# Splitting the Fourier stage by even and odd frequencies, and moving conditioning sums between TensorE and VectorE

## What is computed

```python
sh_m, sc_m, gt_m, sh_f, sc_f, gt_f = jnp.split(silu_c @ w_mod[l] + b_mod[l], N_MOD, axis=-1)
f_x, q_x, k_x, v_x = split_even(modulate(x, g[0], sh_m, sc_m) @ w_in)
attn_x = window_attention(q_x, k_x, v_x, k_c, v_c, sink)
def fourier_mix(u):            # 4 groups of 256 channels, 256 tokens
    ug = u.reshape(b, n, 4, 256)
    return (jnp.fft.fft2(ug, axes=(1, 3)).real * (n * 256) ** -0.5).reshape(b, n, 1024)
mix_x = jnp.concatenate([fourier_mix(f_x), attn_x], axis=-1) @ w_out
```

## Time and profile before

| | |
|---|---|
| median of 3 runs | 2263.23 us (2260.5 to 2265.11) |
| the profiled execution | 2260.15 us, of which its span 2258.4 us |
| PE busy | 2197.8 us (97% of the span) |
| DVE busy | 1653.4 us (73%) |
| ACT busy | 1019.5 us (45%) |
| transfers | 592.63 MB, mean 262 GB/s |
| PE in the chain that ended last | 87% |
| granted clock, mean | 0.989 |

### The profile page before, as it was taken

One profiled execution on the slowest core, in us unless ns is written; L12 is line 12 of the kernel. 1 busy time (PEld: TensorE's weight loads), 2 busy tenths in 40 slices (PEclk: granted clock), 3 DMA queues, 4 the chain that ended last, 5 costly groups with the idle time before them and its releaser, 6 DMA issues.

```text
span 2258.4 us, 30977 instructions
## 1 busy us (share of the span) xinstructions
PE 2197.8 (97%) x11355; PEld 1806.4 (80%) x11355; DVE 1653.4 (73%) x1784; ACT 1019.5 (45%) x1269; POOL 97.7 (4%) x32
## 2 busy tenths in 40 slices
PE   6899999999999999999989999999999999999998
PEld 3478568788888888888868888887888888888887
DVE  0266767888788888888988889988888554654665
ACT  3163544554344345344454444446534443443443
POOL 0000000001010010110101101100011000000000
PEclk8899999999999999999999999999999999999999
DMA  9966978688888888889868788896887656666664
GB/s 374 352 224 226 373 273 298 231 295 278 302 275 285 290 272 292 294 275 318 291 213 279 272 298 280 275 310 226 288 286 247 198 193 189 188 193 193 205 195 149
DMA packets 253896, 592.63 MB, mean 262 GB/s; under 512 B 18082, under 2 KB 18610, under 8 KB 253234
## 3 DMA queue, kind: packets, MB, share of 16 engines
q1 hardware_dynamic: 253746, 590.63, 77.6%
HBM read 588.46 MB, written 2.10 MB: 261 GB/s over the span
## 4 chain that ended last, share of the span: by engine, by line
PE 87%; DVE 5%; DMA 4%; issue 2%; ACT 2%; SPq 1%; DVEq 0%; ACTq 0%
PE ps L520 30%; PE ps L526 15%; PE ps L595 11%; PE ps L596 11%; PE ps L597 11%; PE ps L559 2%; DMA early<-in_w_mod_dram 2%; DVE wlo L1276 1%; DMA mraw<-in_w_mod_dram 1%; DMA raw<-in_mlp_w_dram 1%; DVE acc L1286 1%; PE ps L481 1%; ACT whi L908 1%; DMA raw<-in_att_w_out_dram 1%; PE ps L687 0%
## 5 line engine op out<-in xcount | busy, mean ns | idle before, releaser
L1276 DVE TENSOR_TENSOR wlo<-raw,whi 128x1024 fp32r<-128x1024 f32 x712 | 901.0, 1270 | 429.1 <-ACT whi L908 427.7
L908 ACT ACTIVATE whi<-raw 128x1024 fp32r<-128x1024 f32 x712 | 751.7, 1059 | 946.9 <-PE ps L597 384.6
L520 PE MATMUL ps<-u,whi 128*128 128x512 f32 x2944 | 930.1, 397 | 9.8 <-DVE wlo L1276 5.7
L526 PEld LDWEIGHTS ps<-u,wlo 128*128 128x128 f32 x2944 | 555.1, 189 | 131.5
L526 PE MATMUL ps<-u,wlo 128*128 128x256 f32 x2944 | 580.2, 279 | 0.0
L595 PE MATMUL ps<-whi,h 128*128 128x512 f32 x1216 | 474.6, 390 | 6.9 <-DVE wlo L1276 6.8
L597 PE MATMUL ps<-whi,h 128*128 128x512 f32 x1216 | 473.2, 389 | 0.0
L596 PE MATMUL ps<-wlo,h 128*128 128x512 f32 x1216 | 473.2, 389 | 0.0
L520 PEld LDWEIGHTS ps<-u,whi 128*128 128x128 f32 x2944 | 450.2, 189 | 17.1 <-issue 10.8
L1286 DVE SCALAR_TENSOR_TENSOR acc<-mraw,cs,acc 128x1024 f32<-128x1024 f32 x240 | 306.7, 1278 | 3.9 <-DMA mraw<-in_w_mod_dram 3.9
L595 PEld LDWEIGHTS ps<-whi,h 128*128 128x128 f32 x1216 | 228.3, 188 | 57.3 <-DVE wlo L1276 10.2
(11 more groups left out here) (195 smaller groups left out, 1258.3 us busy)
## 6 DMA issues: line engine op xcount, KB each, us to landing
raw<-in_mlp_w_dram SPq DMA_DIRECT2D x512, 512.0 KB, 4.7
mraw<-in_w_mod_dram SPq DMA_DIRECT2D x272, 512.0 KB, 5.4
early<-in_w_mod_dram SPq DMA_DIRECT2D x96, 512.0 KB, 6.7
raw<-in_conv_w_in_dram SPq DMA_DIRECT2D x96, 512.0 KB, 5.2
raw<-in_att_w_in_dram SPq DMA_DIRECT2D x40, 512.0 KB, 4.4
raw<-in_att_w_out_dram SPq DMA_DIRECT2D x32, 512.0 KB, 6.4
raw<-in_conv_w_out_dram SPq DMA_DIRECT2D x32, 512.0 KB, 6.0
raw<-in_w_mod_dram SPq DMA_DIRECT2D x16, 512.0 KB, 7.1
```

The costliest lines, as they stand in the source:

```text
L520: return pe.matmul(ps[:, 4 * slot + m, :], whi[:, s % SLOTS, cols], src[:, k, :], start=(k == 0), stop=False)
L526: return pe.matmul(ps[:, 4 * slot + m, 0:T], wlo[:, s % SLOTS, cols], src[:, k, 0:T], start=False, stop=(k == KC - 1))
L908: act.activation(whi[:, s, :], raw[:, s, :], ACT.Copy).then_inc(hi_ready, 1)
L1276: dve.tensor_tensor(wlo[:, s, :], raw[:, s, :], whi[:, s, :], ALU.subtract).then_inc(lo_ready, 1)
```

## The change

The Fourier transform of real input is symmetric, and the change uses that: `token_dft` now moves 256 columns instead of 512, the cosines of frequencies 0 to 128 and the sines of 1 to 127 (in `dft` the sine columns are reordered). `channel_dft` multiplies the 129 cosine columns and the 127 sine columns apart, into different columns of PSUM, so its 16 passes have half the columns each. Both halves of the output are then made as difference and sum: ScalarE copies the odd part (2 x 127 columns) and the edges (frequencies 0 and 128), VectorE does one subtraction and one addition (`fourier_sums`), ScalarE rounds the result, VectorE makes the low part.

Of the five first half vectors, four (units 0, 1, 4, 2 in that order) now go through `mraw` on VectorE, 64 slabs in all, and only unit 3 through TensorE, 16 slabs in steps t = 8 to 15. The late sum and its slots are gone. The table `UNITS_BESIDE` gives how many unit slabs VectorE takes with each weight slab: 6 in query group 0, 9 in query group 1, 4 with each of the Fourier slabs 0 to 2, 28 in t = 0 to 16 and 9 in t = 17 to 21. `unit_columns` moves to the start of the loop, t = 4 and t = 22; one `spread_gate` moves to t = 18.

```diff
-MIX_UNITS = (2, 3)
-LATE_UNIT, LATE_SLOTS = 4, 3
+MIX_UNIT = 3
+FIRST_UNITS = (0, 1, 4, 2)
@@ sync
-            for w in range(SL, W_F + 6):
+            for w in range(SL, slab_of(PG_WO) + SL):
                 att_slab(w)
-                for m in FIRST_LOADS.get(w, ()):
-                    first_unit_slab(m)
...
+                for m in units_beside(w - SLOTS):
+                    if m + 2 < len(FIRST_UNITS) * UNIT:
+                        first_unit_slab(m + 2)
+                if w == W_F + 6:
                     sp.wait_ge(slab_used, W_KV + SL)
...
+                for n in MIX_LOADS.get(w - (W_F + 7), ()):
+                    mix_pair(n)
@@ tensor
-                        last = pe.matmul(ps[:, 4 + m, :], fin[:, a, g * T + m * P:g * T + (m + 1) * P], dft[:, a, :],
-                                         start=(a == 0), stop=(a == 1))
+                        last = pe.matmul(ps[:, 4 + m, 0:T], fin[:, a, g * T + m * P:g * T + (m + 1) * P],
+                                         dft[:, a, 1:T + 1], start=(a == 0), stop=(a == 1))
...
+                    for col, lo_n, hi_n in ((P + m * P, P - 1, T), (3 * P * m, 0, P - 1)):
+                        for kc in range(2):
+                            last = pe.matmul(ps[:, g % 2, m * T + lo_n:m * T + hi_n], dft[:, kc, col:col + P],
+                                             ucs[g % 2][kc][:, lo_n:hi_n], start=(kc == 0), stop=(kc == 1))
...
+            unit_columns(0, 6)
             for t in range(24):
...
+                if t == 4:
+                    unit_columns(1, 6)
+                if t == 18:
+                    pe.wait_ge(mix_copied, 1)
+                    pe.wait_ge(m_used, 3 * UNIT)
+                    spread_gate(ones, acc[:, 1, :], 6)
                 if t == 22:
...
+                    unit_columns(2, 2)
@@ out_waits
+                    pe.wait_ge(mod_ready, 3)
+                    spread_gate(first_row, red, 2)
                 if s >= SL // 2:
                     pe.wait_ge(f_ready, s - SL // 2 + 1)
-                if s == SL // 2 + 1:
...
-                    spread_gate(1, 6)
@@ scalar
+                act.activation(odd, two_tiles(g % 2)[:, :, 0:P - 1], ACT.Copy).then_inc(odd_copied, 1)
...
+                act.activation(y_sum[g % 2][:, :, 0:P + 1:P], two_tiles(g % 2)[:, :, P - 1:T:P],
+                               ACT.Copy).then_inc(edges_copied, 1)
...
+                act.activation(u[:, 2 * g:2 * g + 2, 0:T], y_sum[g % 2], ACT.Copy).then_inc(fb_hi, 1)
@@ vector
             for s in range(3):
                 lo(W_F + s, s)
-                first_unit_slab(8 + s)
+                for m in units_beside(W_F + s):
+                    first_unit_slab(m)
...
+                dve.tensor_tensor(y_sum[g % 2][:, :, 1:P], even, odd, ALU.subtract).then_inc(y_summed, 1)
+                dve.tensor_tensor(y_sum[g % 2][:, :, T - 1:P:-1], even, odd, ALU.add).then_inc(y_summed, 1)
...
-                if t < 21:
-                    first_unit_slab(11 + t)
+                for m in units_beside(W_F + 3 + t):
+                    first_unit_slab(m)
@@ tables
-MIX_COPIES = (10, 18)
-LATE_AT = {18: (0, 1), 19: (2, 3), 20: (4, 5), 21: (6, 7, 8), 22: (9, 10, 11), 23: (12, 13, 14), 24: (15,)}
-FIRST_SLABS = (((), (), (), (), (0,), (), (), (1,)), ((2,), (3,), (4,), (5,), (6,), (), (), (7,)))
+MIX_COPY = 16
+MIX_LOADS = {4: (0,), 6: (1,), 8: (2,), 9: (3,), 10: (4,), 11: (5,), 12: (6,), 13: (7,)}
+UNITS_BESIDE = ((0, 1, 1, 0, 1, 1, 1, 1), (1, 1, 1, 0, 2, 1, 1, 2), (4, 4, 4),
+                (2, 2, 1, 2, 1, 2, 2, 2, 1, 2, 1, 2, 2, 2, 1, 2, 1), (2, 2, 2, 2, 1))
```

More of the change, by code:

```diff
@@ L178, in backbone_program @@
         sqj = [ff[:, 2048 + GW * i:2048 + GW * (i + 1)] for i in range(4)]
+        y_sum = [a.rearrange("p (m t) -> p m t", m=2) for a in (tab[:, 260:772], junk[:, :])]
+        odd = diag[:, 0:2, 0:P - 1]
         mt = [fq[:, 8 + 2 * i:10 + 2 * i, :] for i in range(2)]
@@ L677, in fourier_slab, with mix_slab @@
                 last.then_inc(slab_used, 1)
[L679 to L684, removed]
+            def mix_slab(k):
+                if k == 0:
+                    pe.wait_ge(mod_ready, 2)
+                pe.wait_ge(mix_landed[k % SLOTS], 16 * (k // SLOTS + 1))
                 for half in range(2):
@@ L773, in _ @@
                     mix_slab(n)
-                if t == 21:
-                    pe.wait_ge(mix_copied, 2)
-                    pe.wait_ge(m_used, UNIT)
-                if t == 22:
[L778 to L782, removed]
-                pick, rows = ((first_row, mix_row[1]), (ones, late_sum))[i]
-                for n in range(2):
-                    last = pe.matmul(ps[:, bank + n, :], pick, rows[:, n * 512:(n + 1) * 512], start=True, stop=True)
-                last.then_inc(gate_spread, 1)
+                if t == 4:
[4 more added lines that the diff above has]
+                    spread_gate(ones, acc[:, 1, :], 6)
+                if t == 22:
+                    pe.wait_ge(pt_copied, 2 * HEADS)
+                    unit_columns(2, 2)
             def sum_columns(un):
@@ L1604, in _ @@
                     denominator(t - 3)
-                if t < 21:
-                    first_unit_slab(11 + t)
+                for m in units_beside(W_F + 3 + t):
+                    first_unit_slab(m)
+                if t == 6:
+                    finish_first(0, 6)
+                    finish_first(1, 6)
                 if t >= 8 and t % 2 == 0 and t // 2 - 4 < HEADS:
                     o_low(t // 2 - 4)
-                if 0 <= t - 2 * SL < 2 * FG and DFT_ORDER[t - 2 * SL][0]:
-                    fourier_low(DFT_ORDER[t - 2 * SL][1])
-                for k in LATE_AT.get(t, ()):
-                    late_unit_slab(k)
-            finish_first()
+                turned = DFT_ORDER[t - 2 * SL][1] if 0 <= t - 2 * SL < 2 * FG and DFT_ORDER[t - 2 * SL][0] else None
+                if turned is not None:
+                    fourier_sums(turned)
+                if turned is not None:
+                    fourier_low(turned)
+            finish_first(2, 2)
             def gate_units(j):
```

154 lines of the change are left out of this document (69 added, 85 removed).

## The result

| | before | after |
|---|---|---|
| median of four runs each | 2262.22 us (2260.5 to 2265.11) | 2288.52 us (2286.07 to 2289.55) |
| ratio to before, 95% interval | | 1.0121 [1.0103, 1.0139] |
| profiled execution, its span | 2260.15, 2258.4 us | 2289.55, 2287.8 us |
| PE busy | 2197.8 us | 2194.8 us |
| granted clock, mean | 0.989 | 0.979 |

The forecast was 2273.4 us with a range to 2287. The sign and the mechanism came out, the size did not: +26.3 us in the medians and +29.4 between the two profiled spans, where the sum had +10.2. The projection starts at 375.25, where I had looked for it near 355.

What follows compares the result with a forecast made beforehand. The prediction took TensorE to bound the loop, with VectorE's sums, paced by two buffers, next. Its terms, 3.9 + 16.9 + 1.7 - 0.7 - 10.6 - 1.0 = +10.2 us, gave 2273.4 us, range 2258 to 2287.

Steps and rivals of the forecast that it cites:

- query groups: Ahead of the key and value group: three more VectorE sums delay slab 15's low, with nothing covering them; +3.9 us.
- before the loop: Fourier slab 0 through t = 2: unit sums paced by two buffers delay key copy and row maximum; +16.9 us.
- t = 4 to 7: Loop steps 4 to 7: nine sums at 2.95 us, then the Fourier projection's copy, hold TensorE; +1.7 us.
- t = 8 to 15: Loop steps 8 to 15: same TensorE work, 13 sums just covered at a landing of 6.0 us; -0.7 us.
- t = 16 to 23: Loop's end: TensorE has less work, but its last `values` wait for a low behind VectorE's sums; -10.6 us.
- output projection: After the loop: one spread moved out saves 1.7 us, waiting for VectorE's loop end costs 0.7; -1.0 us.
- Rival 3: VectorE fits its sums beside the key and value group, TensorE's 22.4 us come off in full; 2241.5 us, chance 0.13.
- Rival 4: Transforms: 128-column passes held at the weight load's pace, near 3.6 us again; at most 4 us added, chance 0.02.
- Rival 1: Before and in the loop: dearer landings, plus half clock after TensorE idles, 3 us a loss; 2284 us, chance 0.23.
- Rows 10: Trace rows cited for the clock: after a stretch busy 4.0 of 9 us, six us at 0.50, 3 us lost.

Runs made afterwards that it cites:

- e3: The changed kernel with a third buffer for the first 48 unit slabs; 2271.27 us, ratio 1.0052.
- e4: The changed kernel without the loads of the twelve unit slabs beside Fourier slabs 0 to 2, sums kept; 2270.2 us in one run.
- e8: The kernel before with three unused VectorE sums added in query group 0; 2265.45 us in one run.
- e2: The changed kernel with the old full-column transform, so only the unit slabs moved; 2290.93 us, ratio 1.0132.
- e5: The changed kernel with 30 unused matmuls on TensorE at t = 2, 4, 8 and 21; 2285.94 us, ratio 1.0101.
- e1: The kernel before with the new half-column transform alone, all units where they were; 2265.43 us, ratio 1.0011.
- e7: e1 with late slabs moved to t = 20 to 24 and the output projection, their spread later, two unused matmuls at t = 21; 2258.68 us.
- e9: e1 with five unused matmuls at t = 21 and nothing else; 2259.17 us, ratio 0.9985.
- e10: The changed kernel with a third buffer, fewer sums in query group 0 and the second half vector's columns at t = 6; 2267.01 us.
- e11: e10 with four unused matmuls at t = 21; 2268.27 us.

## Why the prediction was off, step by step

The +29.4 us between the two profiled spans, by the prediction's own terms. Without the start phase and the code behind the projection the stage took +26.6 (346.7 us for 320.1) where the sum had +10.2, and the medians differ by 26.3; the step that failed most is the wait ahead of the loop, where idle time was taken as cover, and the next is the clock, which the sum put at nothing.

| term | predicted | measured | how read |
|---|---|---|---|
| start phase, not in the sum | 0 | +2.4 | first query matmul 125.83, 128.27; other kernels here 124.97 to 127.01 with the same code |
| query groups | +3.9 | +3.9 | the four stalls |
| before the loop | +16.9 | +22.4 | row maximum 225.33, 254.03, less the two above |
| t = 4 to 7 | +1.7 | +5.0 | row maximum to t = 8: 26.3, 31.3 |
| t = 8 to 15 | -0.7 | +2.3 | 49.7, 52.0 |
| t = 16 to 23 | -10.6 | -6.4 | 44.4, 38.0 |
| output projection | -1.0 | -0.5 | to the first MLP matmul: 100.2, 99.7 |
| everything later | 0 | +0.3 | spans less the above |

**Right.** The two buffers pace VectorE: twelve sums in 28.6 us where I had 29.0, at a landing of 3.8 where I took 3.9; e3 and e4 showed it by taking the wait away. The query groups cost what was worked out (e8: +3.5 in the kernel before). The transform is halved on TensorE and worth next to nothing beside the units (e2). Rival 3, that TensorE's 22.4 us come off in full, is refuted: the key copy is at 234, not at 208. Rival 4 is too: token and channel transforms take 1.9 us. Rival 1 gave a time within 5 us of the measured one, but in part by luck: its first reason, dear landings before t = 4, did not hold (they are the cheap 3.8), while its clock loss did.

**Before the loop, mis-sized by 5.5 us.** I let VectorE arrive at Fourier slab 0 when ScalarE had it rounded, 3.9 late from the query groups. It arrived at 202.51, 10.2 late: 2.4 from the start phase, 3.9 from query group 0, and 3.8 more from query group 1, for which the sum had no term. The last low of that group that waits for ScalarE, in after and then in before:

```profile
183.94 1.23 DVE L1269 TENSOR_TENSOR wlo<-raw,whi 128x1024 fp32r<-128x1024 f32 x1 [4.55 <-ACT whi L889]
```

```profile
177.59 1.22 DVE L1276 TENSOR_TENSOR wlo<-raw,whi 128x1024 fp32r<-128x1024 f32 x1 [3.35 <-ACT whi L908]
```

Up to here VectorE is only the 6.3 us late that it brought along, since a wait takes up what stands ahead of it. Between this low and Fourier slab 0 stand six sums instead of two: 5.0 us of work more, and 1.5 us of waits for `mraw`. I had seen the 2.73 us of idle time ahead of that low as cover and never set this work against it; 6.5 less 2.7 is the 3.8. And "two slabs are loaded ahead" was not so: the first of the twelve waits 1.76 us, because VectorE had been consuming slabs at the pace of loading until then. From the end of the low to the key copy that makes 30.4 us, not 29.0.

**t = 4 to 7, mis-sized by 3.3 us.** A sum cost 3.3 us, not 2.95. Landings reached 7.6 with a median of 4.6, in the company of the weight slabs. With a third buffer (e3) the same steps took 26.8 us between row maximum and Fourier copy instead of 29.8, so the 3 us go with the third buffer.

**t = 8 to 15, mis-sized by 3.0 us.** I had it just covered. TensorE is busy 50.98 us of 52.0 instead of 49.07 of 49.7; at a mean clock of 0.97 (0.64 in 285.3:290, 1.00 from there on) the same work takes an estimated 1.5 us longer, and idle time grew by 0.4. Between TensorE's first Fourier slab of t = 8 and its first token transform before takes 49.7 us, after 52.1, e3 50.6 and e5, counted behind its unused matmuls, 51.1; in e3 and e5 the clock is 1.00. So 1.0 to 1.5 of the 2.4 us go with the clock. In after, TensorE then waits 0.73 us for VectorE's copy of the Fourier projection at the end of this part (337.37), so the sums have a share too; the rest stays open. The -0.7 that I had credited to this part did not come.

**t = 16 to 23, mis-sized by 4.2 us.** The wait for the last low part came as worked out, at 28.2 us into the stretch instead of 26.5, 1.7 late. What I left out is what follows it: 9.7 us instead of 7.3, because `values` and a channel transform ran at half clock or little above it (3.75 for 1.89, 2.83 for 1.95). The clock stood in the prediction as a rival, priced at 3 us for a single loss. Rows 10 showed the very thing, and I gave it no place in the likeliest sum though that sum itself had TensorE idle for 5 to 12 us three times. The Trainium skill, "TensorE: Matmul & The Clock Gate", part 1, says that idling takes the clock down, and the trace agrees (0.50 behind the 3.68 us here and the 5.18 us of e1); I should have put it into the main case wherever TensorE sets the end behind a wait, which is at the end of the loop. Where VectorE sets it, in t = 0 to 7, leaving it out was right: e5.

**What stays open.** The start phase differs by up to 3.3 us between kernels in which it is the same code, and what lies behind the projection takes 1808.9 to 1816.1 us in the profiled executions of these kernels, though nothing is changed there; neither is put down to the change. e4 and e8 rest on one run each. And of the 14 us of matmul that the transform saves, e7 and e9 keep 4 and 3 in the medians and none up to the MLP in their profiled executions: the output projection takes them back, by waits for lows at 426 and 430 and a clock of 0.83 in 420:440 (e7). Of these two lows in e9, the first stands behind VectorE's own work (a unit sum and the gating of the output, without idle time from 422.78), the second right behind ScalarE's rounding (428.02 to 429.08), which had waited 3.75 us for the slab. The queue in turn had waited 14.8 us for VectorE's sums and 7.0 for its lows (405:432), before and e9 nearly alike. No run changes either, so what would give TensorE's lead a use there is not shown; nor is where the 3 and 4 us lie.

## What to carry to other kernels

Before work is moved to an engine that is busy only 73% of the time, work out the pace of its supply: with N buffers, one item costs the larger of its own time and (landing + item) / N, and here that is an estimated 2.6 us (3.8 for the landing, 1.28 for the sum, 0.1 for the issue, two buffers) against 1.28, and 2.4 was measured (28.6 us for twelve); a third buffer in an unused tile gave 17 of the 26 us back. Then count every item between the last wait and the point at which another engine needs the result, and subtract it from the idle time seen there instead of taking that as cover. And a cut on the bounding engine can be lost whole in the next wait; look first at what it will wait for, then at its clock behind that wait.

## What the runs showed of the hardware

In one place the half clock (a granted clock of 0.50, the 1.2 GHz level) lasted much longer than I expected, and under full load. In e1 a wait of 5.18 us, late in a loop in which TensorE had been busy 14.4 of 15 us at a clock of 1.00 (300:315), was followed by 0.50 from 330 to 345 with TensorE busy 15.00 of 15 us. Its thin columns still took double at 345.95, and the matmuls of the projection took 0.63 us instead of 0.39 until 353.2, over 24 us behind the wait.

Elsewhere it was short. Behind the 3.68 us wait of after (365.54) the clock was 0.50 for 3.6 us, 0.65 for the next 2.6, and 1.00 from 371.7; behind the 3.08 us wait of e10 (340.79) it was 1.00 again from 344. One difference is in what TensorE did: in e1 the thin columns came right behind `values` and then alternated with channel transforms, in after and e10 a channel transform came first. No run tests that.

The length of the wait alone does not tell whether the clock falls. In e9 a wait of 0.80 us (327.54) was followed by 1.00, but waits of 1.95 and 1.46 us (426.58 and 430.39) by 0.50 in 428:434; in e11 a wait of 0.94 us (346.67) was followed by 0.50 in 350.8:353. Behind the 2.83 us wait of after at 285.29 the clock was 0.64 up to 290 and then 1.00, but it had been low before that wait too. Five matmuls whose result nobody reads, put in place of e1's wait, were worth 6.3 us in the medians. Why the half clock of e1 lasted so long, the record does not say.
